# Recurrent heads of a two-block kernel: decay rows by transposing a broadcast column, key and query lengths one head ahead, inner masks moved, no drain at modulation products

## The reference

```python
q, k, v = l2_norm(heads(q)), l2_norm(heads(k)), heads(v)
...
gc = jnp.cumsum(g.reshape(b, h, nc, CHUNK), axis=-1)
diff = gc[..., :, None] - gc[..., None, :]
decay = jnp.where(tril, jnp.exp(jnp.where(tril, diff, 0.0)), 0.0)
lower = jnp.where(strict, jnp.einsum('bhnik,bhnjk->bhnij', k_beta, kc) * decay, 0.0)
t_inv = lax.linalg.triangular_solve(eye + lower, ...)
u = t_inv @ v_beta
w = t_inv @ (k_beta * jnp.exp(gc)[..., None])
intra = jnp.where(tril, jnp.einsum('bhnik,bhnjk->bhnij', qc, kc) * decay, 0.0)
q_dec = qc * jnp.exp(gc)[..., None]
```

## Time and profile before

| | us |
|---|---|
| median of three runs | 2708.47 |
| lowest and highest | 2707.21, 2708.78 |
| span of the profiled execution, first to last instruction | 2705.5 |
| eight heads, from the first key transposes to the last modulation products | 72.5 to 592.7 |
| PE, DVE, ACT, POOL busy in the whole span | 2639.9, 1005.3, 832.5, 801.9 |

### The profile page before, as it was taken

One profiled execution on the slowest core, in us unless ns is written; L12 is line 12 of the kernel. 1 busy time (PEld: TensorE's weight loads), 2 busy tenths in 40 slices (PEclk: granted clock), 3 DMA queues, 4 the chain that ended last, 5 costly groups with the idle time before them and its releaser, 6 DMA issues.

```text
span 2705.5 us, 35632 instructions
## 1 busy us (share of the span) xinstructions
PE 2639.9 (98%) x14540; PEld 1979.1 (73%) x14540; DVE 1005.3 (37%) x1837; ACT 832.5 (31%) x1460; POOL 801.9 (30%) x643
## 2 busy tenths in 40 slices
PE   7999999999999999999999899999999999999998
PEld 4777777886558885544453797988888987988887
DVE  3656566623432153222121696300011786200012
ACT  3444444423433241000000427322223336322222
POOL 2222223320114430000000342344455433444453
PEclk9999999999999999999999899999999999999999
DMA  7122222001104229999999321232222221233221
GB/s 276 53 65 71 77 74 62 31 26 61 46 30 141 94 80 372 426 427 426 426 427 425 121 86 47 79 94 94 95 98 88 94 79 48 78 95 106 96 94 47
DMA packets 189046, 382.41 MB, mean 141 GB/s; under 512 B 11889, under 2 KB 146933, under 8 KB 163317
## 3 DMA queue, kind: packets, MB, share of 16 engines
q1 hardware_dynamic: 187712, 379.59, 37.8%
q10 hardware_dynamic: 1205, 0.99, 0.1%
HBM read 378.46 MB, written 2.10 MB: 141 GB/s over the span
## 4 chain that ended last, share of the span: by engine, by line
PE 89%; DVE 4%; ACT 3%; DMA 1%; issue 1%; SPq 1%; DVEq 1%; POOL 0%; ACTq 0%
PE bank L1684 14%; PE bank L1689 14%; PE bank L1688 14%; PE bank L1974 12%; PE bank L1452 5%; PE bank L1921 2%; PE bank L1486 2%; PE bank L1548 2%; PE bank L1557 1%; PE bank L1738 1%; PE bank L1561 1%; PE bank L1467 1%; DMA place<-in_w_down 1%; PE bank L1755 1%; PE bank L1660 1%
## 5 line engine op out<-in xcount | busy, mean ns | idle before, releaser
L755 POOL TENSOR_TENSOR w_lo<-ring,w_hi 128x512 fp32r<-128x512 f32 x384 | 521.6, 1390 | 671.5 <-ACT w_hi L805 671.5
L805 ACT ACTIVATE w_hi<-ring 128x2048 fp32r<-128x2048 f32 x96 | 184.0, 1917 | 622.9 <-PE bank L1684 622.9
L1684 PE MATMUL bank<-hT_hi,w_hi 128*128 128x512 f32 (+1 forms) x928 | 352.7, 380 | 3.4 <-DVE conv_acc L2913 1.6
L1689 PE MATMUL bank<-hT_hi,w_lo 128*128 128x512 f32 (+1 forms) x928 | 347.8, 375 | 0.0
L1688 PE MATMUL bank<-hT_lo,w_hi 128*128 128x512 f32 (+1 forms) x928 | 347.6, 375 | 0.0
L1684 PEld LDWEIGHTS bank<-hT_hi,w_hi 128*128 128x128 f32 x928 | 174.8, 188 | 35.4 <-DVE hT_lo L2815 2.0
L1689 PEld LDWEIGHTS bank<-hT_hi,w_lo 128*128 128x128 f32 x928 | 174.7, 188 | 31.7
L1688 PEld LDWEIGHTS bank<-hT_lo,w_hi 128*128 128x128 f32 x928 | 174.9, 188 | 30.6 <-issue 1.0
L3006 DVE TENSOR_TENSOR ffn_hT<-ffn_sg,bank 128x512 f32<-128x512 f32 x44 | 30.3, 688 | 414.8 <-PE bank L1689 414.8
L755 POOL TENSOR_TENSOR w_lo_m<-ring,w_hi_m 128x512 fp32r<-128x512 f32 x64 | 82.4, 1320 | 302.3 <-ACT w_hi_m L805 302.3
L1452 PE MATMUL bank<-hT,head_w 128*128 128x512 f32 x336 | 156.9, 593 | 0.0
(11 more groups left out here) (525 smaller groups left out, 5239.7 us busy)
## 6 DMA issues: line engine op xcount, KB each, us to landing
ring<-in_w_gate SPq DMA_DIRECT2D x56, 1024.0 KB, 7.7
ring<-in_w_down SPq DMA_DIRECT2D x52, 1024.0 KB, 7.8
ring<-in_w_up SPq DMA_DIRECT2D x46, 1024.0 KB, 8.6
place<-in_w_up SPq DMA_DIRECT2D x40, 1024.0 KB, 18.3
place<-in_w_down SPq DMA_DIRECT2D x34, 1024.0 KB, 24.9
ring<-in_w_in SPq DMA_DIRECT2D x33, 1024.0 KB, 5.2
place<-in_w_gate SPq DMA_DIRECT2D x30, 1024.0 KB, 23.9
head_w<-in_w_in SPq DMA_DIRECT2D x32, 512.0 KB, 4.9
```

The costliest lines, as they stand in the source:

```text
L755: last = pool.tensor_tensor(w_lo[m % 2][:, cs], src[:, cs], w_hi[m % 2][:, cs].bitcast(F32), ALU.subtract)
L805: return act.activation(dst, src, ACT.Copy)
L1684: first = mm(dst, a[0], b[0], start=start, stop=False)
L1689: return mm(dst, a[1], b[0], start=False, stop=stop)
```

## The change

The decay rows come from a transpose of `head_q[:, 1]` (minus the running sum), broadcast to 128 columns in the operand itself; `g_wide` goes, and ACT's Exp and Abs take scale -1. PE does this first in a head, as soon as `head_q` is there. The key transposes and query lengths of head h+1 move into head h, between the scan and the z projection; for head 0 they stand in front of `project_z(0)`. ACT takes the squares and roots of the next head's lengths at the end of the previous head, and starts a head with the decay; `v_tok` is copied after `knT`. POOL's `intra` masks move behind level 2. DVE forms the second decayed query after the product with key-key. PE no longer drains after mod2; the last four products increment `mod2_done` each, and its readers count in fours.

```diff
@@ SP
-                sp.wait_ge(sem("mod2_done"), h - 1)
+                sp.wait_ge(sem("mod2_done"), h * 4 - 4)
...
@@ POOL
-                for d in range(2):
-                    pool.wait_ge(sem("decay_ready"), h * 2 + d + 1)
-                    pool.tensor_tensor(intra[:, d], decay[:, d], tri[:, d:d + 1, :].to_broadcast([P, TT, P]), ALU.mult)\
-                        .then_inc(sem("intra_masked"), 1)
                 pool.wait_ge(sem("l_ready"), h + 1)
                 level(0)
...
                 level(1)
                 level(2)
+                for d in range(2):
+                    in_turn(pool, f"decay_ready_{d}", h)
+                    pool.tensor_tensor(intra[:, d], decay[:, d], tri[:, d:d + 1, :].to_broadcast([P, TT, P]), ALU.mult)\
+                        .then_inc(sem("intra_masked"), 1)
@@ ACT
-            def head(h, more):
+            def key_squares(h):
+
                 act.wait_ge(sem("tok_done"), h * 2 + 1)
                 for t in range(TT):
                     act.activation(solve_N[:, t, :], bank[4][:, t * P:(t + 1) * P], ACT.Square, accum_out=ss[:, 4 + t:5 + t])
-                act.drain()
-                in_turn(act, "q_len_done", h)
+
+            def lengths(h):
+
+                act.wait_ge(sem("q_len_done"), h + 1)
                 act.activation(rms[:, 0:4], bank[3][:, 0:4], ACT.Sqrt, bias=eps_col[:, 0:1])
                 act.activation(rms[:, 4:8], ss[:, 4:8], ACT.Sqrt, bias=eps_col[:, 0:1]).then_inc(once_a_turn["len_ready"], 1)
+
+            def head(h, more):
+                for d in range(2):
+                    act.wait_ge(sem("gc_row_done"), h * 2 + d + 1)
+                    act.activation(e_row[:, d, :], bank[6 + d][:], ACT.Exp, scale=-1.0).then_inc(once_a_turn[f"e_row_ready_{d}"], 1)
+                    for t in range(TT):
+                        act.activation(decay[:, d, t, :], bank[6 + d][:, t * P:(t + 1) * P], ACT.Abs, scale=-1.0,
+                                       bias=head_q[:, 1, 2 * t + d:2 * t + d + 1])
+                    act.drain()
+                    act.activation(flat_rows(decay[:, d]), flat_rows(decay[:, d]), ACT.Exp, scale=-1.0).then_inc(once_a_turn[f"decay_ready_{d}"], 1)
+                act.wait_ge(sem("kT_done"), h + 1)
+                copy(knT[:], bank[4][:]).then_inc(sem("kT_ready"), 1)
                 act.wait_ge(sem("tok_done"), h * 2 + 2)
                 copy(flat_rows(v_tok[:]), bank[5][:]).then_inc(once_a_turn["v_tok_ready"], 1)
...
                     q_squared()
+                    key_squares(h + 1)
...
                 if more:
+                    lengths(h + 1)
                     convolved(h + 1, 2)
...
             convolved(0, 2)
+            key_squares(0)
+            act.drain()
+            lengths(0)
             take_z(0)
@@ PE
-                to_tokens(1, 4)
-
-                pe.wait_ge(sem("head_done"), h + 1)
-                to_tokens(2, 5)
-                pe.wait_ge(sem("q_sq_ready"), h + 1)
-                for t in range(TT):
-                    last = mm(bank[3][:, t:t + 1], q_sq[:, tiles[t]], all_ones[:, 0:1], start=True, stop=True)
-                last.then_inc(once_a_turn["q_len_done"], 1)
-                in_turn(pe, "g_wide_ready", h)
+                in_turn(pe, "head_q_ready", h)
                 for d in range(2):
                     for t in range(TT):
-                        last = mm(bank[6 + d][:, tiles[t]], g_wide[:, t, d, :], tri[:, d, :], start=True, stop=True)
+                        last = pe.transpose(bank[6 + d][:, tiles[t]], head_q[:, 1, 2 * t + d:2 * t + d + 1].to_broadcast([P, P]), ident[:])
                     last.then_inc(sem("gc_row_done"), 1)
+                pe.wait_ge(sem("head_done"), h + 1)
+                to_tokens(h, 2, 5)
                 fill(0, 0, KD)
...
                 last.then_inc(sem("o_done"), 1)
+                if more:
+                    to_tokens(h + 1, 1, 4)
+                    query_squares(h + 1)
...
-                    mm(bank[0][g * 32:g * 32 + 32, :], silu_cb[:, k, :], mod2_w[:, k, :], start=k < 4, stop=k >= 4)
-                pe.drain().then_inc(sem("mod2_done"), 1)
+                    last = mm(bank[0][g * 32:g * 32 + 32, :], silu_cb[:, k, :], mod2_w[:, k, :], start=k < 4, stop=k >= 4)
+                    if k >= 4:
+                        last.then_inc(sem("mod2_done"), 1)
...
+            to_tokens(0, 1, 4)
+            query_squares(0)
             project_z(0)
@@ DVE
-                copy(g_wide[:].rearrange("p t d n -> p (t d) n"), head_q[:, 4, :].unsqueeze(2).to_broadcast([P, TT * 2, P]))\
-                    .then_inc(once_a_turn["g_wide_ready"], 1)
...
+                def decayed_queries(d):
+
+                    in_turn(dve, f"e_row_ready_{d}", h)
+                    tt(q_decT[:, d, :], conv_out[:, 0, :], e_row[:, d, :], ALU.mult).then_inc(sem("q_dec_ready"), 1)
+
                 for d, dst in enumerate((l_neg, l_bwd)):
-                    dve.wait_ge(sem("e_row_ready"), h * 2 + d + 1)
-                    tt(q_decT[:, d, :], conv_out[:, 0, :], e_row[:, d, :], ALU.mult).then_inc(sem("q_dec_ready"), 1)
-                    dve.wait_ge(sem("decay_ready"), h * 2 + d + 1)
+                    in_turn(dve, f"decay_ready_{d}", h)
                     for t in range(TT):
                         stt(dst[:, t, :], decay[:, d, t, :], head_q[:, 0, 2 * t + d:2 * t + d + 1], strict_neg[:, d, :], ALU.mult, ALU.mult)
+                    if d == 0:
+                        decayed_queries(0)
...
                 tt(flat_rows(l_neg[:]), flat_rows(l_neg[:]), bank[3][:], ALU.mult).then_inc(sem("l_ready"), 1)
+                decayed_queries(1)
...
-                dve.wait_ge(sem("mod2_done"), h + 1)
+                dve.wait_ge(sem("mod2_done"), h * 4 + 4)
```

More of the change, by code:

```diff
@@ L166, in build @@
         w_small = at("w_small", r.pos - 4096, [P, KD, 96])
-        g_wide = at("g_wide", r.pos - 4096, [P, TT, 2, P])
         mod1_part = at("mod1_part", r.pos, [P, 4, 512])
@@ L407, in build @@
             "head_vector": (
-                "head_q_ready", "g_wide_ready", "k_tok_ready", "intra_ready", "o_ready", "mod2_copied",
+                "head_q_ready", "k_tok_ready", "intra_ready", "o_ready", "mod2_copied",
             ),
             "head_tensor": (
-                "q_len_done", "kk_done", "kq_done", "oT_done",
+                "kk_done", "kq_done", "oT_done",
             ),
             "head_scalar": (
-                "z_ready", "len_ready", "v_tok_ready", "o_rms",
+                "len_ready", "z_ready", "v_tok_ready", "o_rms",
+            ),
+            "head_decay": (
+                "e_row_ready_0", "decay_ready_0", "e_row_ready_1", "decay_ready_1",
             ),
@@ L583, in _ @@
                 load_z(h)
-                sp.wait_ge(sem("mod2_done"), h - 1)
+                sp.wait_ge(sem("mod2_done"), h * 4 - 4)
                 load_mod2(h - 1)
-            sp.wait_ge(sem("mod2_done"), HEADS - 1)
+            sp.wait_ge(sem("mod2_done"), 4 * (HEADS - 1))
             load_mod2(HEADS - 1)
@@ L915, in head @@
                     act.activation(solve_N[:, t, :], bank[4][:, t * P:(t + 1) * P], ACT.Square, accum_out=ss[:, 4 + t:5 + t])
-                act.drain()
-                in_turn(act, "q_len_done", h)
+            def lengths(h):
+                act.wait_ge(sem("q_len_done"), h + 1)
                 act.activation(rms[:, 0:4], bank[3][:, 0:4], ACT.Sqrt, bias=eps_col[:, 0:1])
                 act.activation(rms[:, 4:8], ss[:, 4:8], ACT.Sqrt, bias=eps_col[:, 0:1]).then_inc(once_a_turn["len_ready"], 1)
+            def head(h, more):
[9 more added lines that the diff above has]
+                copy(knT[:], bank[4][:]).then_inc(sem("kT_ready"), 1)
                 act.wait_ge(sem("tok_done"), h * 2 + 2)
                 copy(flat_rows(v_tok[:]), bank[5][:]).then_inc(once_a_turn["v_tok_ready"], 1)
-                for d in range(2):
-                    act.wait_ge(sem("gc_row_done"), h * 2 + d + 1)
-                    act.activation(e_row[:, d, :], bank[6 + d][:], ACT.Exp).then_inc(sem("e_row_ready"), 1)
-                    for t in range(TT):
[L926 to L931, removed]
                 if more:
@@ L1490, in _, with to_tokens, query_squares @@
             tiles = [slice(t * P, (t + 1) * P) for t in range(TT)]
-            def head(h, more):
[L1495 to L1499, removed]
+            def to_tokens(h, s, b):
+                pe.wait_ge(sem("silu_done"), h * 3 + s + 1)
+                for c in tiles:
+                    last = pe.transpose(bank[b][:, c], conv_out[:, s, c], ident[:])
+                last.then_inc(sem("tok_done"), 1)
+            def query_squares(h):
+                pe.wait_ge(sem("q_sq_ready"), h + 1)
+                for t in range(TT):
+                    last = mm(bank[3][:, t:t + 1], q_sq[:, tiles[t]], all_ones[:, 0:1], start=True, stop=True)
+                last.then_inc(sem("q_len_done"), 1)
+            def head(h, more):
                 def fill(s, k0, k1):
```

1 line of the change is left out of this document (removed).

## The result

The changed kernel takes 2714.4 us (median of 11 runs, 2711.1 to 2717.3) against 2708.5 for the kernel before (11 runs, 2706.8 to 2711.0): a ratio of 1.0024, 95% interval 1.0016 to 1.0031. It is slower by 5.9 us, 0.24%; the forecast was 2712.7 with a range of 2706 to 2719. Its profiled execution took 2712.8 us with a span of 2710.9, 5.4 over the span before (2705.5).

A forecast was written before the change was run, and what follows sets the result against it. PE, busy 98% of the 2705.5 us span, was taken as the bound. Terms +4.8 + 2.4 - 4.0 + 1.0 = +4.2 us gave a span of 2709.7 and, with 3.0 carried, 2712.7 us; range 2706 to 2719.

The forecast's parts named there:

- idle at the first head: Ahead of head 0, PE waits for ACT's Silus because key transposes and lengths precede z: 4.8 us later, paid once.
- the clock behind it: After the new idle of 6.2 us at the start, PE runs at a lower granted clock: 2.4 us, range 0 to 2.9.
- head boundaries: At each of seven boundaries the query projection starts 0.57 us earlier: gain 4.0 us, range 2.6 to 5.4.
- masks beside the convolution: POOL's moved masks take turns with DVE, fourth solve_X slips 0.15 us: 1.0 us over 7 heads, bounds 0 to 8.9.
- the shortest idle with a low clock behind it: PE idle of 2.41 us in the earlier trace, cited for a boundary idle of 1.1 us leaving the clock alone.
- The 3.0 us from span to median: Difference between the earlier profiled span and the three-run median 2708.47, added to the predicted span 2709.7 to give 2712.7 us.
- DVE's release: At the head boundary without the drain, mod2's last product frees DVE 1.92 + 0.04 us after the start, not 2.13.
- my 1.03 us from the copy to the transposes: At the head boundary, head_q is complete 1.00 us after DVE's mod2 copy begins, plus 0.03 to reach PE's decay transposes.
- Rival 1: POOL's masks hold DVE by a whole mask, 1.27 us in seven heads: +12.1 us, 2720.6, slower; chance 0.17.
- Rival 2: In the decay rows, the broadcast column loads slowly, as a matmul does: +12.0 us, 2720.5; chance 0.05.
- Rival 3: At head boundaries no wait for head_q, and the clock stays up: -5.9 us, 2702.6, faster; chance 0.05.
- Rival 4: At head boundaries, transposes and drain removal gain nothing PE sees, while the prologue cost stays: +8.2 us, 2716.7; chance 0.08.

The follow-up runs named there:

- e7_warm_idle: Changed kernel with 27 extra 128x128 products, results overwritten, filling PE's idle ahead of head 0: 2711.3 us, ratio 1.0009 to the kernel before.
- e6_masks_back: Changed kernel with POOL's two intra masks back ahead of level 0: 2713.9 us, ratio 1.0022 to the kernel before; head period 64.73 us.
- e2_head_q_early: Changed kernel, but DVE copies the next head's head_q before waiting for the modulation products: 2704.7 us, ratio 0.9985 to the kernel before; head period 63.50 us.
- run 32: Not a follow-up run: the words say that PE, in the kernel before, had executed 32 products of one column (619.74 to 623.4).
- e4_transposes_only: Kernel before with only the decay rows by transposing the broadcast column, no wide copy, signs in ACT's scale: 2700.5 us, ratio 0.9971.
- e9_no_drain_only: Kernel before with only PE's drain behind the modulation products gone: 2706.4 us, ratio 0.9992; head period 64.77 us.
- e13_one_increment: Changed kernel, but only the last of eight modulation products increments the semaphore, by four: 2715.1 us in one run; head period 64.71 us.

## Why the prediction was right, point by point

*The sum.* Predicted +4.2 us, measured +5.4 in the profiled span and +5.9 in the median. The mechanisms were right; one term, the gain at the boundaries, was about half of what I forecast and lies outside its own range. Each term has its own measurement:

| term | predicted | measured |
|---|---|---|
| idle at the first head | +4.8 | +4.95 (e7_warm_idle) |
| the clock behind it | +2.4, 0 to 2.9 | +2.35 in this profile, to 3.45 in others |
| head boundaries | -4.0, -2.6 to -5.4 | -2.1 |
| masks beside the convolution | +1.0, 0 to 8.9 | +0.5 (e6_masks_back: 7 x 0.07), made up for elsewhere in the head |
| not forecast | | -0.3 ahead of the start, -0.2 last drain, +0.7 behind the heads |

*The start.* Right in place, mechanism and size: PE idle from 65.2 to 71.2 for ACT's Silu, the fill at 83.70 where I had about 84.

*The clock.* Right, and the upper bound of 2.9 was too low: e2_head_q_early's profile has 3.45. What I wrote of the shortest idle with a low clock behind it, 2.41 us, is no lower bound: in the kernel before the granted clock is also 0.50 from about 624.5 to 627.5, and PE has no idle listed there; it had run 32 products of one column (619.74 to 623.4) and then a projection of full tiles. The changed kernel's runs spread over 6.2 us and those of the kernel before over 4.2; the profiles show that a part of this is the clock at the start, but I did not trace the rest. The mean granted clock of the changed kernel's runs was 0.993 to 0.995, that of the profiled one 0.995, and its time is 1.6 us under the median. The 3.0 us from span to median that I carried were of the same kind: a run's time is about 1.9 us over its own span, so the other 1.1 must be by how much the profiled execution of the kernel before lay under its median. The difference of the two is the 0.5 between +5.4 and +5.9.

*The head boundary.* The mechanism was the one measured: the drain's gain turns into a wait for `head_q`, 1.22 us where I said some 1.1, and transposes at half price. The size of the gain, 0.57 us a head, was too high by 0.24: what had taken 13.84 us takes 13.51 (7.76 from z to the products, 4.50 to the fill, 1.25 moved ahead of z). The rest of the head is as long as before, with the masks' 0.07 in it. The step that was mis-sized is DVE's release, "1.92 + 0.04 us after the start": it was 2.18. That took 0.22; my 1.03 us from the copy to the transposes was 0.96 and gave 0.07 back. The z projection takes 7.23 us instead of 7.14, in every kernel here with the lengths moved in front of it and in no other, a further 0.09 of which I found no cause. At the seventh boundary I had counted a gap of 0.63 us where there were 0.38.

*The masks.* I expected turns, and 0.15 us a head at the fourth solve_X; the turns are there, the place is right, and it is 0.07. Rival 1 (a whole mask per head) fell with e6_masks_back. Rival 2 (slow broadcast load) fell with e4_transposes_only, 0.90 us for the eight. Rival 3 (no wait, full clock) fell with the profile itself; e2_head_q_early shows that it was one edit away. Rival 4 (nothing gained in the heads) fell with the period of 64.80, though the gain is nearer to the middle between it and the forecast than to the forecast.

*The chances.* At +0.24% (0.16 to 0.31) the result lies just past the 0.2% that I had set as the edge of "same", which I held the likelier at 0.56 against 0.38 for slower. In the span 1.2 us are missing. The boundary term fell short by 1.9 us (-2.1 for -4.0), and 1.0 of that came back because the head behind the boundary is as long as before where I had added 1.0 for the masks; that part is luck. The start, the clock and what was not forecast make up the other 0.3.

*Not tried:* the shift of the lengths alone on the kernel before, the new order of DVE and ACT by itself, and any version with a different cover for the Silu at the start.

## What to carry to other kernels

When independent work is moved out of the stretch in front of a wait, look at what the wait is for: here 1.25 us of work left the stretch, and 1.22 us of waiting came in, for a 0.2 us copy that stood behind a 0.6 us copy on DVE. Transposes and no drain, with nothing moved, gave 13 us instead of a loss of 6. A loop's steady state is not the whole price: moving work one turn ahead puts it in front of the first turn too, where its input may just be in the making. Here that was an idle of 6 us on the matrix engine, and the low clock behind it cost 2.3 to 3.45 us more. Copy small operands of the next turn while the engine that makes them is idle, not behind the turn's last large copy.

## What the runs showed of the hardware

- A transpose whose stationary operand is one column broadcast with step 0 costs 0.11 us in a stream of them (0.90 for eight, e4_transposes_only), half of an fp32 128 x 128 product's 0.23 (1.87 for eight, before). Its weight load takes 137 ns, a dense one's 140.
- A drain of PE between independent work showed as 0.63 us of "issue" at the loop's end; without it the next transposes started 1.86 us after the products' start instead of 2.56 (e9_no_drain_only). Where no jump of the loop follows it is 1.85 instead of 2.31.
- Four increments by products that run side by side release the waiting engine 0.07 us later than one increment of four (2.18 against 2.11, e13_one_increment).
- After 5.99 us without work PE's granted clock was 0.50 until about 76.8 us, 5.6 us into the new work; over five profiles of kernels with this start this cost 2.3 to 3.45 us.
- DVE and POOL take turns here: beside POOL's masks two taps took 0.58 and 1.59 us, and beside a POOL scaling a tap took 1.30 us that takes 0.75 alone. Moving two masks of 1.27 us there cost 0.07 us a head (e6_masks_back).
